# A two-layer hybrid encoder on one core: the input in five pieces on two queues, the second weight split in halves, a later load of the third, and a turn of values put behind a projection

## What is computed

```python
def even_layer(x, norm_w, w_in, w_out, ...):
    h = rmsnorm(x, norm_w)
    proj = jnp.einsum('bsd,de->bse', h, w_in)
    qa, ka, va, ga, qh, ffw, fbw, ih, gh = split_cols(proj, EVEN_SIZES)
    oa = differential_attention(qa, ka, va, ...) * jax.nn.silu(ga)
    ob = hgrn2_bidirectional(qh, ffw, fbw, ih, ...) * jax.nn.silu(gh)
    return jnp.einsum('bse,ed->bsd', jnp.concatenate([oa, ob], axis=-1), w_out)
```

## Time and profile before

| | |
|---|---|
| median of three runs | 1115.86 us (1115.53 to 1117.06) |
| the profiled execution's own time | 1116.22 us |
| its span, first to last instruction | 1114.5 us |
| PE busy | 1092.1 us (98% of the span) |
| DVE busy | 967.5 us (87%) |
| ACT busy | 679.8 us (61%) |
| mean granted TensorE clock | 0.995 |

### The profile page before, as it was taken

One profiled execution on the slowest core, in us unless ns is written; L12 is line 12 of the kernel. 1 busy time (PEld: TensorE's weight loads), 2 busy tenths in 40 slices (PEclk: granted clock), 3 DMA queues, 4 the chain that ended last, 5 costly groups with the idle time before them and its releaser, 6 DMA issues. The chain is left out here.

```text
span 1114.5 us, 18506 instructions
## 1 busy us (share of the span) xinstructions
PE 1092.1 (98%) x5690; PEld 910.8 (82%) x5690; DVE 967.5 (87%) x1956; ACT 679.8 (61%) x1310; POOL 0.2 (0%) x4
## 2 busy tenths in 40 slices
PE   8999999999999999999999999999999999999996
PEld 7778888888888888888888877888888888888875
DVE  6879989889889889889889898889888888988886
ACT  6475665654654654654654665366677666677764
POOL 0000000000000000000000000000000000000000
PEclk9999999999999999999999999999999999999998
DMA  8614423324224224225125201563232324323111
GB/s 231 171 38 112 135 76 95 95 75 105 84 75 112 76 75 122 66 75 131 57 75 148 79 20 50 122 160 104 86 94 56 94 68 124 103 65 94 57 39 76
DMA packets 132634, 103.67 MB, mean 93 GB/s; under 512 B 5488, under 2 KB 118512, under 8 KB 132592
## 3 DMA queue, kind: packets, MB, share of 16 engines
q1 hardware_dynamic: 131760, 102.28, 33.4%
q10 hardware_dynamic: 832, 0.85, 0.2%
HBM read 77.95 MB, written 2.10 MB: 72 GB/s over the span
## 5 line engine op out<-in xcount | busy, mean ns | idle before, releaser
L75 PE MATMUL bank_proj<-hH,w_hi 128*128 128x512 f32 x856 | 341.5, 399 | 1.1 <-DVE w_lo L1335 1.1
L77 PE MATMUL bank_proj<-hH,w_lo 128*128 128x512 f32 x856 | 334.4, 391 | 0.0
L76 PE MATMUL bank_proj<-hL,w_hi 128*128 128x512 f32 x856 | 334.3, 391 | 0.0
L77 PEld LDWEIGHTS bank_proj<-hH,w_lo 128*128 128x128 f32 x856 | 160.8, 188 | 34.9
L75 PEld LDWEIGHTS bank_proj<-hH,w_hi 128*128 128x128 f32 x856 | 161.2, 188 | 32.2 <-DVE w_lo L1335 2.0
L76 PEld LDWEIGHTS bank_proj<-hL,w_hi 128*128 128x128 f32 x856 | 161.3, 188 | 29.9 <-issue 0.2
L2111 ACT ACTIVATE probs<-probs,small 128x256 f32<-128x256 f32 (+1 forms) x128 | 71.2, 559 | 54.8 <-DVE small L2379 54.4
L1335 DVE TENSOR_TENSOR w_lo<-w_raw,w_hi 128x1024 fp32r<-128x1024 f32 x73 | 88.5, 1220 | 0.9 <-ACT w_hi L797 0.7
L2118 ACT ACTIVATE probsT<-bank_odd_turn 128x256 fp32r<-128x256 f32 (+1 forms) x128 | 49.1, 435 | 64.0 <-PE bank_odd_turn L1834 63.5
L797 ACT ACTIVATE w_hi<-w_raw 128x1024 fp32r<-128x1024 f32 x73 | 77.0, 1055 | 0.2
L926 ACT ACTIVATE scaled<-decay 128x1024 f32<-128x1024 f32 x32 | 34.0, 1064 | 61.8 <-PE bank_score L611 59.6
(11 more groups left out here) (464 smaller groups left out, 2159.5 us busy)
## 6 DMA issues: line engine op xcount, KB each, us to landing
w_raw<-in_w_in_even SPq DMA_DIRECT2D x71, 512.0 KB, 4.8
w_raw<-in_w_in_odd SPq DMA_DIRECT2D x36, 512.0 KB, 4.3
qs<-parts SPq DMA_DIRECT2D x96, 128.0 KB, 2.3
ks<-parts SPq DMA_DIRECT2D x40, 256.0 KB, 4.5
o_raw<-in_w_out_even SPq DMA_DIRECT2D x15, 512.0 KB, 5.9
o_raw<-in_w_out_odd SPq DMA_DIRECT2D x14, 512.0 KB, 6.6
mixT<-in_x SPq DMA_DIRECT2D x4, 256.0 KB, 5.9
rope<-in_rope SPq DMA_DIRECT2D x2, 512.0 KB, 6.5
```

The costliest lines, as they stand in the source:

```text
L75: pe.matmul(out, hi, moving_hi, start=start, stop=False)
L76: pe.matmul(out, hi, moving_lo, start=False, stop=False)
L77: return pe.matmul(out, lo, moving_hi, start=False, stop=stop)
```

## The change

x comes in five pieces, of 1, 1, 2, 2 and 2 k-tiles. ACT now issues the second half of four of them (832 KB with the identity matrix, 576 KB before). The third weight (n = 0) is issued only when all of x has landed, and the tables stand behind it. The nine matmuls of ones become 7, 6 and 4 ahead of the turns of k-tiles 0, 1 and 2. PE takes one k-tile of the first projection ahead of each later turn, and turns the sums of squares one k-tile later. The second weight is split into high and low parts in two halves. On DVE the low part of weight 1 moves into the query's rotation, ahead of its parts, and that of weight 2 into the key's. PE's turn of `vt` moves behind projection 2.

```diff
-WARM = 9
+WARM = (7, 6, 4, 0)
+PIECES = ((0, 1), (1, 2), (2, 4), (4, 6), (6, 8))
...
             load_half(0, half_landed)
             load_x(0, 1)
+            load_x(0, 2)
             load_half(4, w_in_sem[0])
-            for i in (2, 3):
-                for a in range(2):
-                    load_x(a, i)
+            load_x(0, 3)
+            load_x(0, 4)
+            load_x(1, 4)
             load(0, -1)
+            sp.wait_ge(x_landed[-1].sem, x_landed[-1].at(0, 2))
+            load(0, 0)
             sp.dma_start(rope[:], rope_d).then_inc(rope_landed.sem, DMA)
-            load(0, 0)
...
-            for c in range(WARM):
-                pe.matmul(PB[1][:, 0:P], ones, ones, start=True, stop=True)
             for k in range(4):
+                for c in range(WARM[k]):
+                    pe.matmul(PB[1][:, 0:P], ones, ones, start=True, stop=True)
                 turn_x(k)
...
-            proj(0, -2, 0, 1)
-            turn_x(4)
-            turn_x(5)
-            proj(0, -2, 1, 2)
-            turn_x(6)
-            proj(0, -2, 2, 3)
-            turn_x(7)
-            proj(0, -2, 3, 4)
+            for k in range(4):
+                proj(0, -2, k, k + 1)
+                turn_x(k + 4)
             proj(0, -2, 4)
-            proj(0, -1, 0, 5)
+            proj(0, -1, 0, 4)
+            proj(0, -1, 4, 6)
...
-            proj(0, -1, 5)
+            proj(0, -1, 6)
...
             pe.wait_ge(x_kept[0].sem, x_kept[0].at(0, 3))
-            pe.wait_ge(PB[2].free.sem, PB[2].free.at(0, 0))
-            turn(0, 1, vt)
 
             def iteration(h, first, last):
 
                 proj(h, 2)
+                if first:
+                    pe.wait_ge(PB[2].free.sem, PB[2].free.at(0, 0))
+                    turn(0, 1, vt)
...
-            for i in range(2):
-                part = x[2 * P:4 * P, 2 * i * P:2 * (i + 1) * P].rearrange("(t p) d -> p t d", p=P)
+            for i in range(4):
+                cols = slice(PIECES[i][0] * P, PIECES[i][1] * P)
+                part = x[2 * P:4 * P, cols].rearrange("(t p) d -> p t d", p=P)
...
-            high_x(1)
+            high_half(0, 0, half_high)
+            for k in range(1, 4):
+                high_x(k)
             act.wait_ge(w_in_sem[0].sem, w_in_sem[0].at(0, 0))
-            act.activation(w_hi[0][:, 4:KT], w_raw[0][:, 4:KT], ACT.Copy).then_inc(w_high.sem, 1)
+            high_half(0, 4, w_high)
+            high_x(4)
             keep_first_x()
-            for k in range(2, KT):
+            for k in range(5, KT):
                 high_x(k)
-            high(0, -1)
+            act.wait_ge(w_in_sem[1].sem, w_in_sem[1].at(0, 0))
+            high_half(1, 0, half_high)
+            high_half(1, 4, w_high)
...
-            def rotate(h, n):
+            def rotate(h, n, between=None):
...
                 dve.tensor_tensor(turned[:, 0], turned[:, 0], turned[:, 1], ALU.add).then_inc(roped.sem, 1)
+                if between is not None:
+                    low(*between)
                 dve.wait_ge(roped.sem, roped.at(h, i + 3))
...
-            low(0, -1)
+            dve.wait_ge(half_high.sem, half_high.at(0, 2))
+            low_half(1, 0, half_low)
+            dve.wait_ge(w_high.sem, w_high.at(0, -1))
+            low_half(1, 4, w_low)
...
-            rotate(-1, 7)
-            low(0, 1)
-            rotate(-1, 8)
+            rotate(-1, 7, between=(0, 1))
+            rotate(-1, 8, between=(0, 2))
             scale_vt(0, 0, 0)
-            low(0, 2)
             last_lambda()
```

More of the change, by code:

```diff
@@ L230, in even_layer @@
         KEPT = (1, 2, 5, 3, 4)
-        x_landed = [sem(f"x_landed{i}", unit=DMA) for i in range(4)]
+        x_landed = [sem(f"x_landed{i}", unit=DMA) for i in range(len(PIECES))]
         eye_landed = sem("eye_landed", unit=DMA)
@@ L455, in turn_x @@
                     pe.wait_ge(eye_landed.sem, eye_landed.at(0, 1))
-                if k % 2 == 0:
-                    pe.wait_ge(x_landed[k // 2].sem, x_landed[k // 2].at(0, 2))
+                for i, (first, _) in enumerate(PIECES):
+                    if k == first:
+                        pe.wait_ge(x_landed[i].sem, x_landed[i].at(0, 2))
                 if k == 6:
@@ L476, in proj @@
                 bank, use = bank_of(n)
-                if n == -2 and first == 0:
-                    pe.wait_ge(half_low.sem, half_low.at(0, 1))
-                elif first == 0 or n == -2 and first <= 4 < end:
+                if n in (-2, -1) and first == 0:
+                    pe.wait_ge(half_low.sem, half_low.at(0, n + 3))
+                elif first == 0 or n in (-2, -1) and first <= 4 < end:
                     pe.wait_ge(w_low.sem, w_low.at(h, n))
@@ L940, in _, with high_half @@
             act.wait_ge(norm_landed.sem, norm_landed.at(0, 1))
+            def high_half(s, first, count):
+                part = slice(first, first + 4)
+                act.activation(w_hi[s][:, part], w_raw[s][:, part], ACT.Copy).then_inc(count.sem, 1)
             high_x(0)
             act.wait_ge(half_landed.sem, half_landed.at(0, 1))
[L943 to L944 removed]
+            high_half(0, 0, half_high)
+            for k in range(1, 4):
+                high_x(k)
             act.wait_ge(w_in_sem[0].sem, w_in_sem[0].at(0, 0))
[L946 removed]
+            high_half(0, 4, w_high)
+            high_x(4)
             keep_first_x()
[L948 removed]
+            for k in range(5, KT):
                 high_x(k)
[L950 removed]
+            act.wait_ge(w_in_sem[1].sem, w_in_sem[1].at(0, 0))
+            high_half(1, 0, half_high)
+            high_half(1, 4, w_high)
             for t, into in enumerate((decay, soft, turned, probs)):
[L952 to L953 removed]
+                for landed_piece in x_landed:
+                    act.wait_ge(landed_piece.sem, landed_piece.at(0, 2))
                 act.activation(into[:, :, :].rearrange("p a t -> p (a t)"), x_tiles[t // 2][:, t % 2, :], ACT.Square,
@@ L1361, in _, with low_half @@
             low_x = lambda k: raw.split_low(dve, k, XB[k][:])
+            def low_half(s, first, count):
+                part = slice(first, first + 4)
+                dve.tensor_tensor(w_lo[s][:, part], w_raw[s][:, part], w_hi[s][:, part].bitcast(F32),
+                                  ALU.subtract).then_inc(count.sem, 1)
             low_x(0)
             dve.wait_ge(half_high.sem, half_high.at(0, 1))
-            dve.tensor_tensor(w_lo[0][:, 0:4], w_raw[0][:, 0:4], w_hi[0][:, 0:4].bitcast(F32),
-                              ALU.subtract).then_inc(half_low.sem, 1)
-            low_x(1)
+            low_half(0, 0, half_low)
+            for k in range(1, 4):
+                low_x(k)
             dve.wait_ge(w_high.sem, w_high.at(0, -2))
-            dve.tensor_tensor(w_lo[0][:, 4:KT], w_raw[0][:, 4:KT], w_hi[0][:, 4:KT].bitcast(F32),
-                              ALU.subtract).then_inc(w_low.sem, 1)
+            low_half(0, 4, w_low)
             keep_x(KEPT[0])
-            for k in range(2, KT):
+            for k in range(4, KT):
                 low_x(k)
-            low(0, -1)
+            dve.wait_ge(half_high.sem, half_high.at(0, 2))
+            low_half(1, 0, half_low)
+            dve.wait_ge(w_high.sem, w_high.at(0, -1))
+            low_half(1, 4, w_low)
             for k in KEPT[1:]:
```

10 lines of the change are left out of this document (4 added, 6 removed).

## The result

The changed kernel takes **1119.61 us** (median of 14 runs, 1118.77 to 1120.03); the kernel before, on the same chip, 1116.72 (14 runs). The ratio is 1.0026, 95% interval [1.0018, 1.0033]: **slower by 2.9 us**, where 1.8 had been forecast. The 1115.86 us on which the forecast stood are the median of the first three of these 14 runs. The time lies in the predicted range, but on the other side of the 0.2% that had been taken as the limit of what can be told.

What follows compares the result with a forecast made beforehand. PE, busy 98% of the span, bounds the kernel. Gains of 1.07 + 0.49 + 0.5 us are lost in two waits, leaving a 1.8 us lag: 1115.86 + 1.8 = 1117.7 us, range 1115.8 to 1119.8.

Steps and rivals of the forecast that it cites:

- The key's wait: Ahead of the first scores: the inserted low part delays query and key moves, so PE waits 2.1 us for the key.
- The moved turn: Turn of vt: ACT's copy 4.01 us later, the softmax chain behind it equally late; PE lags 1.8 us at second scores.
- The second rival: Softmax chain: ACT and DVE make up the moved turn's 4 us; lag only 0.5, time 1116.3; chance 14%.
- smaller pieces and a second queue change the order, not the sum: Loading of x: k-tile 4 still lands at 10.3, is turned then instead of 11.12; PE leads 1.07 us by projection -1.
- The price of the second queue and of smaller pieces: Loading of x: cost between nothing and 0.8 us, the latter with k-tile 4 turned at 11.12; taken as nothing.
- The root: Behind the sums' turn, one k-tile (0.70) later on PE: root, tables' scaling and DVE's rotations lead by 0.37 us.
- The clock: Beginning: feeding PE evenly, with ones in gaps, removes the 1.2 GHz stretch where two turns and a k-tile took 3.05 us.
- the first rival: At k-tile 1: late landing idles PE, the clock falls again; lag 3.6, time 1119.5; chance 22%.
- The baseline: Whole kernel before: 1.8 us lag added to the 1115.86 median; the profiled execution, 1116.22, stood 0.36 over it.
- The wait at the second scores: Second scores: PE waits about 1.3 us, released by ACT's softmax; no wait there would mean the forecast is wrong.
- the late turn of k-tile 4 (after 11): Beginning: k-tile 4 was to be turned near 10.3; a turn after 11 would mean the forecast is wrong.
- Terms at nothing: Third weight held until x is in: lands at 18.3, wanted about 20, 2 us of cover, so no cost.

Runs made afterwards that it cites:

- run without insertion: Changed kernel with the low parts of weights 1 and 2 back behind the rotations, turn of values still late: 1120.72 us, ratio 1.0039.
- filled run: Changed kernel with twelve unused products of ones on PE ahead of the first scores, in the wait for the key: 1118.60 us, ratio 1.0027.
- order of turns back: Beginning alone, with k-tiles 5 and 6 of x turned one projection tile earlier, as in the kernel before: 1117.25 us, ratio 1.0010.
- rotations and turn alone: Kernel before with only the low parts inside the rotations and the turn of values behind projection 2: 1119.26 us, ratio 1.0028.
- beginning alone: Changed kernel with the turn of values and the low parts both put back, rest of the change kept: 1116.52 us, ratio 1.0002.
- pieces back: Beginning alone, with x in four pieces on the queues and in the order of before: 1116.49 us, ratio 1.0001.
- order and sums back: Order of turns back, plus the sums' turn put back ahead of the sixth k-tile of projection -1: 1116.31 us, ratio 1.0005.
- copy behind the gates: Changed kernel with ACT's copy of the turned values moved behind the first gate's functions and weight 4's high part: 1118.37 us, ratio 1.0023.
- before with ones: Kernel before with ten unused products of ones ahead of the turn of x's k-tile 2: 1115.51 us, ratio 0.9998.

## Why the prediction was right, and where not

- **The key's wait: right.** Forecast 2.1 us, found 2.35. The low part ahead of the query's parts delays their moves, and the key's behind them. The price of that insertion with the turn in its old place is 1117.71 - 1116.52 = 1.2 us. With the turn behind projection 2 it saves about as much (1120.72 to 1119.61, in two sessions).
- **The moved turn: right, and the larger term.** Forecast: the copy 4.01 us later, the softmax chain rigid behind it. Found: the copy 5.19 later, a chain of 8.60 to 8.66 us in six profiles, and 4.26 once the copy was cut out of it. Without the insertion the move costs 1120.72 - 1116.52 = 4.2 us, with it 1.9 (1119.61 - 1117.71, in two sessions; 1.3 by the ratios): the insertion lets projection 1 start 1 us earlier (29.64 against 30.58) and with it the turn. The second rival, "only the key binds", fell with the run without insertion.
- **The step that failed: "smaller pieces and a second queue change the order, not the sum ... The turn of k-tile 4 moves from 11.12 to 10.3 ... PE leads by 1.07 us."** It was turned at 11.46, and projection -1 started at 18.12, not 16.8. The landing of 10.31 in the earlier trace rows was one execution's, and the sum did change: 0.61 MB moved in the first 5 us against the 0.84 of the earlier trace rows, and 2.19 against 2.53 MB in the first 10; the 0.34 MB missing are 1.0 us at 336 GB/s. SP's half of k-tiles 4 and 5 landed at 11.41 (3.80 + 7.6). PE wasn't ready for it earlier either: k-tile 1 had landed at 8.34 instead of about 7, k-tiles 2 and 3 at 9.75, and the first three matmuls, which were to be done by 10.3, started their last at 11.20. All later marks are late by that error: projection 1 by 1.3 (29.64 for 28.33), the key by 1.4 (43.47 for 42.1), the second bank of scores by 1.1 (51.32 for 50.21). This is 1.1 of the 1.9 us by which the profile's lag at projection 4, 3.69, exceeds the 1.8 forecast. Most of the rest is the half clock: from the filled run, where projection 4 starts 0.62 us behind the release of that bank (51.65 against 50.83 + 0.20), it would start here at 51.94 and not at 52.59, an estimate of 0.65.
- **The price of the second queue and of smaller pieces** was bounded by 0 and 0.8 and taken as 0. In the five kernels with four pieces the later half of k-tiles 4 and 5 landed between 10.07 and 11.38, in the nine with five pieces between 10.66 and 11.41; the means are 10.67 and 11.03, about 0.4 apart, less than the spread from run to run. The bytes of the first 5 us don't overlap: 0.72 to 0.89 MB with four pieces, 0.57 to 0.69 with five. Whether the smaller pieces or the second queue's longer list do it was not taken apart. The Trainium skill, "DMA: Bandwidth & Descriptors", section "Queues, rings and completion order", has each engine serve the queues with work in turn; by that ACT's list delays SP's. The 8.34 of k-tile 1's SP half, with 1.01 us of idle ahead of it, fits that and doesn't prove it.
- **The root: half right.** The sums' turn was expected 0.37 earlier and came 0.93 later. That one k-tile more ahead of it costs was said; the two runs with the order of turns back point to its eating what earlier squares gain (1117.25 with the k-tile, 1116.31 without it), in two sessions.
- **The clock: right kind, wrong place.** The half clock did leave the beginning. It came back behind a wait, but the wait for the key, not for k-tile 1, and so the first rival's 1119.5 was close for another reason: in the changed kernel that fall costs only 0.5 or so. The range reached up to 1119.8 for that rival's sake; the time lies outside the 1116.9 to 1118.6 that the forecast gave itself, so that it is in the range at all is partly luck.
- **The baseline.** The sum was made against an execution with the half clock, which two thirds of the runs of before don't have, and its median of three runs, 1115.86, is 0.9 under that of all 14. Against runs with a whole clock (1115.4 to 1116.0 by session) the beginning has nothing to win from the clock, and the change loses some 4 us.
- **The wait at the second scores** was named as a mark, and the profile after doesn't have it; like the late turn of k-tile 4 (after 11), its absence was to say that the forecast is wrong. The wait was hidden: at half speed PE reached the scores at 51.68, behind the end of both exponentials (51.32). It stands in the run of rotations and turn alone (0.70) and in the filled one (0.38).
- **Terms at nothing.** The held third weight was in at 17.22, and ACT took it at 21.34 straight behind the squares, without a wait: right.

What stays open is the half to nearly two microseconds by which the four kernels with the new beginning, or parts of it, and nothing else stand over the runs of before with a whole clock in their own sessions (beginning alone 0.5, pieces back 1.1, order of turns back 1.9, order and sums back 0.9). Pieces and order of turns were each put back, and the sums' turn with the latter; none restored the whole. The halves of the second weight (n = -1) and the held tables were not tried by themselves.

## What to carry to other kernels

Before an instruction is moved later because its consumer "had been waiting anyway", look at what is queued behind that consumer on its engine: here a 0.6 us copy stood at the head of an 8.6 us chain in program order, and 5 us of delay went straight through it. With the copy out of that order the second scores no longer waited. And two waits that overlap don't add up: take each away alone, and then both, before one of them gets the blame.

## What the hardware did that was not expected

- The granted clock doesn't follow the length of one idle time. A wait of 2.35 us for the key was followed by 0.50 in the profile after, one of 2.42 in the run with the copy behind the gates was not; before, 1.81 us ahead of k-tile 2 was followed by it, and 2.65 in the run of rotations and turn alone was not. The Trainium skill, "TensorE: Matmul & The Clock Gate", section "HAM oscillation — how this bites in real kernels", ties the fall to waits for a DMA that are longer than the stretches of matmuls between them. The traces agree that it falls behind a wait for a DMA, but here the key's wait of 2.35 us had 11 us of matmuls without an idle time ahead of it (29.64 to 40.66). And by the mean clocks of their runs (0.996 in four and 0.997 or 0.998 in four with the copy behind the gates) the same kernel drops the clock in some executions only.
- Ten or twelve products of ones in a wait kept PE's clock: all 18 runs of the two kernels that differ by them alone (before with ones, key wait filled) have a mean granted clock of 0.997 or 0.998.
